# A decoder step: constants issued by GpSimd, eight stage buffers for w_out, the first merged tile in two parts, output stores issued by SyncE

## The reference

```
h = RMSNorm(x);  z = h @ w_in          # pool 512 | 3 x (q, k, v) | gate_pool 1024 | gate_attn 1024
A = (pooling mixer of z) @ w_branch_pool
B = (dilated sliding attention, 3 head groups) @ w_branch_attn
merged = sigmoid(gate_pool) * A + sigmoid(gate_attn) * B
x += RMSNorm(merged @ w_out)
up = RMSNorm(x) @ ffn_w_up;  act = gelu(conv(up)_a) * conv(up)_b
y = x + RMSNorm(act @ ffn_w_down)
```

## Time and profile before

| | |
|---|---|
| three timed runs | 1652.8, 1654.02, 1658.04 us; median 1654.02 us |
| profiled execution | 1652.44 us, of which the span from first to last instruction is 1650.8 us |
| mean granted TensorE clock | 0.982 |
| busy share of the span | PE 97%, PE weight loads 90%, DVE 44%, ACT 33%, POOL 9% |
| chain that ended last | PE 94%, DVE 3%, ACT 1%, issue 1% |

### The profile page before, as it was taken

How to read it: one execution, slowest core, us unless ns; L and a number is a source line. 1 busy time by engine, 2 the same in 40 slices (tenths; PEclk the granted TensorE clock), 3 DMA queues, 4 the chain that set the end, 5 groups by cost and what they waited for, 6 DMA issues and landing times.

```text
span 1650.8 us, 24555 instructions
## 1 busy us (share of the span) xinstructions
PE 1597.7 (97%) x9631; PEld 1485.9 (90%) x9631; DVE 731.7 (44%) x1205; ACT 550.7 (33%) x1058; POOL 146.3 (9%) x193
## 2 busy tenths in 40 slices
PE   6999999999999999979999999999999999999996
PEld 6889999999999999968889999999999998888774
DVE  6474563656322232245444343434343435464533
ACT  7233231333221231133333333333333334343432
POOL 0123242330000000000000000000000000000000
PEclk9999999999899999999999999999999999999998
DMA  7134355340423422040036654655542217565550
GB/s 248 54 107 149 116 186 189 108 148 27 140 77 112 121 91 74 16 164 18 0 107 211 196 175 157 212 191 177 161 150 66 82 48 260 178 218 175 201 164 29
DMA packets 143107, 218.91 MB, mean 133 GB/s; under 512 B 13121, under 2 KB 115953, under 8 KB 142136
## 3 DMA queue, kind: packets, MB, share of 16 engines
q1 hardware_dynamic: 132423, 190.99, 36.5%
q0 software_dynamic: 9648, 26.01, 4.2%
q10 hardware_dynamic: 969, 0.99, 0.2%
HBM read 192.14 MB, written 70.02 MB: 159 GB/s over the span
## 4 chain that ended last, share of the span: by engine, by line
PE 94%; DVE 3%; ACT 1%; issue 1%; DMA 0%; ACTq 0%; POOL 0%; POOLq 0%; DVEq 0%
PE PS L987 48%; PE PS L1195 16%; PE PS L882 9%; PE PS L1123 6%; PE PS L867 4%; PE PS L1051 2%; PE PS L939 2%; PE PS L911 1%; PE PS L925 1%; PE PS L1095 1%; PE PS L895 1%; PE PS L849 0%; PE PS L1132 0%; DMA wo_stage<-in_w_out 0%; PE PS L1002 0%
## 5 line engine op out<-in xcount | busy, mean ns | idle before, releaser
L1729 DVE TENSOR_TENSOR tw_lo<-tw_stage,tw_hi 128x1024 fp32r<-128x1024 f32 x72 | 86.5, 1202 | 415.7 <-ACT tw_hi L1336 415.5
L987 PE MATMUL PS<-h_hi,tw_hi 128*128 128x352 f32 x1032 | 226.1, 327 | 0.0
L987 PE MATMUL PS<-h_hi,tw_lo 128*128 128x352 f32 x1032 | 222.4, 323 | 0.0
L987 PE MATMUL PS<-h_lo,tw_hi 128*128 128x352 f32 x1032 | 221.9, 323 | 0.0
L987 PEld LDWEIGHTS PS<-h_hi,tw_lo 128*128 128x128 f32 x1032 | 176.8, 188 | 0.0
L987 PEld LDWEIGHTS PS<-h_lo,tw_hi 128*128 128x128 f32 x1032 | 175.1, 188 | 0.0
L987 PEld LDWEIGHTS PS<-h_hi,tw_hi 128*128 128x128 f32 x1032 | 173.6, 189 | 0.4
L1995 DVE TENSOR_TENSOR wd_lo<-wd_stage,wd_hi 128x1024 fp32r<-128x1024 f32 x66 | 80.8, 1225 | 137.9 <-ACT as_hi L1526 136.7
L1336 ACT ACTIVATE tw_hi<-tw_stage 128x1024 fp32r<-128x1024 f32 x72 | 72.8, 1012 | 206.7 <-PE PS L987 200.2
L2018 DVE SCALAR_TENSOR_TENSOR cacc<-cext,cols,cacc 128x1024 f32<-128x1024 f32 x88 | 113.0, 1285 | 56.5 <-ACT cacc L1550 27.7
L1195 PE MATMUL PS<-wd_hi,as_hi 128*128 128x512 f32 (+1 forms) x396 | 123.1, 392 | 1.1 <-ACT cnat L1559 1.1
(11 more groups left out here) (253 smaller groups left out, 2717.3 us busy)
## 6 DMA issues: line engine op xcount, KB each, us to landing
wd_stage<-in_ffn_w_down SPq DMA_DIRECT2D x66, 512.0 KB, 3.5
tw_stage<-in_ffn_w_up SPq DMA_DIRECT2D x44, 512.0 KB, 3.9
out_k_s<-in_cache_k_w SPq DMA_DIRECT2D x8, 2044.0 KB
out_v_s<-in_cache_v_w SPq DMA_DIRECT2D x8, 2044.0 KB
qb<-zs SPq DMA_DIRECT2D x24, 512.0 KB, 5.1
acts<-cact POOLq DMA_DIRECT2D x22, 528.0 KB, 8.5
tw_stage<-in_w_in SPq DMA_DIRECT2D x20, 512.0 KB, 5.7
as_stage<-acts SPq DMA_DIRECT2D x44, 192.0 KB, 3.7
```

Of the source, the lines that this page charges most:

```text
L987: last = pe.matmul(PS[:, bank + b, 0:BW], w[s][:, k, :], x[:, k, b * BW:(b + 1) * BW], start=(k == 0 and j == 0), stop=(k == kc - 1 and j ...
L1729: dve.tensor_tensor(tw_lo[s][:, 0:kc, :], tw_stage[s][:, 0:kc, :], tw_hi[s][:, 0:kc, :].bitcast(F32), ALU.subtract).then_inc(tw_lo_done, 1)
```

## The change

1. The eight constants are issued by POOL, just behind the `eps` memset, and no longer by ACT. ACT takes a root of `eps` into a cell that is overwritten later, so that the table with the root is the first one loaded.
2. w_out has eight stage buffers: four new ones lie where `ba_stage` and `tw_stage` were, and are loaded once these have been read (`ba_split` 2; `tw_lo_done` 29 and 30). The loads of x follow behind all eight; the last one waits for four blocks of w_out instead of eight, and the first load of ffn_w_up for all eight.
3. Tile 0 of merged has a place of its own (`mg_first`) and is split in two parts, blocks 0 to 5 and 6 to 7. ACT copies the first part during the last gate block; all eight `split_wo` stand together behind the last gate. PE's tile 0 waits for `ba_used` 7 besides, since the banks that it writes are read by `gated_attn(6)`.
4. At the end DVE multiplies PSUM by the gain as soon as the sum of squares is there, takes the reciprocal, and does the scaling and the addition of x in one instruction. `ytmp` has three buffers. SP issues the stores: three behind load 30, three behind load 52, three at the end.

```diff
@@ SBUF places and buffers
+        BA_STAGE = Y + 2 * 4 * T
+        wo_stage += [at(o)(f"wo_stage{4 + i}", [P, D]) for i, o in enumerate((BA_STAGE, BA_STAGE + 4 * D, TW, TW + 4 * D))]
...
+        mg_first = at(TW + 4 * KC * P * 2)("mg_first", [P, KC, P], F32R)
...
-        ytmp = [sb1(f"ytmp{s}", [P, D]) for s in range(2)]
+        ytmp = [sb1(f"ytmp{s}", [P, D]) for s in range(3)]
@@ sync
             for k in range(KC):
-                if k == KC - 1:
-                    sp.wait_ge(ba_done, KC)
-                    load_x(0)
-                if k >= 4:
-                    sp.wait_ge(wo_lo_done, k - 3)
-                sp.dma_start(wo_stage[k % 4][:, :], w_out[:, k, :]).then_inc(qw_in[k % 4], 16)
+                if k == 4:
+                    sp.wait_ge(ba_split, 2)
+                if k >= 6:
+                    sp.wait_ge(tw_lo_done, 2 * PAIR_UP + k - 6 + 1)
+                sp.dma_start(wo_stage[k][:, :], w_out[:, k, :]).then_inc(qw_in[k] if k < 4 else xr_in[k - 4], 16)
+            sp.wait_ge(ba_done, KC)
+            load_x(0)
             load_x(1)
-            sp.wait_ge(wo_lo_done, KC)
+            sp.wait_ge(wo_lo_done, 4)
             load_x(2)
             sp.dma_start(xnat[0:TS, 8, :], xs).then_inc(x_in[2], 16)
+            sp.wait_ge(wo_lo_done, KC)
...
+            def store_y(n):
+                sp.wait_ge(y_ready, n + 1)
+                dst, part = (ys, slice(0, TS)) if n == 8 else (yp[n * P:n * P + P], slice(0, P))
+                sp.dma_start(dst, ytmp[n % 3][part, :]).then_inc(y_out[n % 3], 16)
             for q in range(NWD, len(DOWN)):
                 load_down(q)
+                if q % FC == 8 and q > FC:
+                    for x in range(3):
+                        store_y(3 * (q // FC - 1) + x)
+            for n in range(6, NTILE):
+                store_y(n)
@@ gpsimd
             pool.memset(eps[:, :], EPS).then_inc(pool_set, 1)
+            for dst, src in ((mask[:, :], io["c_mask"].rearrange("p b k -> p (b k)")), (smask[:, :], io["c_smask"]), (count[:, :, :], io["c_count"]),
+                             (par_a[0:16, :], io["b_gate"][0].rearrange("(j p) -> j p", p=P)),
...
+                pool.dma_start(dst, src).then_inc(const_in, 16)
...
-            for n in range(NTILE):
-                pool.wait_ge(y_ready, n + 1)
-                dst, part = (ys, slice(0, TS)) if n == 8 else (yp[n * P:n * P + P], slice(0, P))
-                pool.dma_start(dst, ytmp[n % 2][part, :]).then_inc(y_out[n % 2], 16)
@@ tensor
                     if n == 0:
                         pe.wait_ge(wo_lo_done, k + 1)
-                        pe.wait_ge(mg_done, 1 if k < KC - 1 else 2)
-                    hi, lo = mg_hi[n % 2][:, k, 0:rows], mg_lo[:, k, t0:t0 + rows]
+                        pe.wait_ge(mg_done, 1 if k < KC - 2 else 2)
+                    if n == 0 and k == 0:
+                        pe.wait_ge(ba_used, KC - 1)
+                    hi, lo = (mg_hi[n % 2] if n else mg_first)[:, k, 0:rows], mg_lo[:, k, t0:t0 + rows]
@@ scalar
             act.dma_start(gb[:, :], io["norm_mix_pre"][0].partition_broadcast(P)).then_inc(gain_in, 16)
-            for dst, src in ((mask[:, :], io["c_mask"].rearrange("p b k -> p (b k)")), (smask[:, :], io["c_smask"]), (count[:, :, :], io["c_count"]),
...
-                act.dma_start(dst, src).then_inc(const_in, 16)
+            act.wait_ge(pool_set, 1)
+            act.activation(rms[:, 0, 0:1], eps[:, 0:1], ACT.Sqrt)
...
-            act.wait_ge(pool_set, 1)
             square(0)
...
                 if j < KC - 2:
                     split_tw(PAIR_GA + j // 2 + 1, j % 2, KC)
-            for k in range(3):
+                if j == KC - 2:
+                    act.wait_ge(tp_done[0], PAIR_UP)
+                    act.wait_ge(sum_done, KC - 2)
+                    act.activation(mg_first[:, 0:KC - 2, :], merged[:, 0:KC - 2, 0:P], ACT.Copy).then_inc(mg_hi_done, 1)
+            for k in range(KC):
                 split_wo(k)
...
-            act.wait_ge(sum_done, KC - 1)
-            act.activation(mg_hi[0][:, 0:KC - 1, :], merged[:, 0:KC - 1, 0:P], ACT.Copy).then_inc(mg_hi_done, 1)
-            for k in range(3, KC):
-                split_wo(k)
             act.wait_ge(sum_done, KC)
-            act.activation(mg_hi[0][:, KC - 1, :], merged[:, KC - 1, 0:P], ACT.Copy).then_inc(mg_hi_done, 1)
+            act.activation(mg_first[:, KC - 2:KC, :], merged[:, KC - 2:KC, 0:P], ACT.Copy).then_inc(mg_hi_done, 1)
@@ vector
+            low_first(0, KC - 2, 1)
             low_wo(0)
+            low_wo(1)
             gated_attn(KC - 2)
...
@@ vector, last stage, for each tile
+                    rows = tile_of(n)[1]
+                    dve.wait_ge(o_ss, 9 + n + 1)
+                    if G:
+                        dve.wait_ge(y_out[x], 16 * G)
+                    dve.tensor_tensor(ytmp[x][0:rows, :], PS[0:rows, 2 * pair:2 * pair + 2, :].rearrange("p b n -> p (b n)"),
+                                      gfin[0:rows, :], ALU.mult).then_inc(f_free, 1)
                     dve.wait_ge(o_rms, 9 + n + 1)
-                    rows = tile_of(n)[1]
                     dve.reciprocal(prstd[0:rows, 1, n:n + 1], prms[0:rows, 1, n:n + 1]).then_inc(f_step, 1)
                     dve.wait_ge(f_step, n + 1)
-                    dve.wait_ge(y_out[n % 2], 16 * (n // 2))
-                    dve.scalar_tensor_tensor(ytmp[n % 2][0:rows, :], PS[0:rows, 2 * pair:2 * pair + 2, :].rearrange("p b n -> p (b n)"),
-                                             prstd[0:rows, 1, n:n + 1], gfin[0:rows, :], ALU.mult, ALU.mult).then_inc(f_free, 1)
                     dve.wait_ge(f_free, n + 1)
-                    dve.tensor_tensor(ytmp[n % 2][0:rows, :], ytmp[n % 2][0:rows, :], xnat[0:rows, n, :], ALU.add).then_inc(y_ready, 1)
+                    dve.scalar_tensor_tensor(ytmp[x][0:rows, :], ytmp[x][0:rows, :], prstd[0:rows, 1, n:n + 1], xnat[0:rows, n, :],
+                                             ALU.mult, ALU.add).then_inc(y_ready, 1)
```

More of the change, by code:

```diff
@@ L488, in build @@
         y_ready = sem("y_ready")
-        y_out = [sem(f"y_out{s}") for s in range(2)]
+        y_out = [sem(f"y_out{s}") for s in range(3)]
         state_out = sem("state_out")
@@ L1440, in split_wo @@
             def split_wo(k):
-                act.wait_ge(qw_in[k % 4], 16 * (4 * NG + k // 4 + 1))
-                act.activation(wo_hi[:, k, :], wo_stage[k % 4][:, :], ACT.Copy).then_inc(wo_hi_done, 1)
+                if k < 4:
+                    act.wait_ge(qw_in[k], 16 * (4 * NG + 1))
+                else:
+                    act.wait_ge(xr_in[k - 4], (80, 48, 48, 48)[k - 4])
+                act.activation(wo_hi[:, k, :], wo_stage[k][:, :], ACT.Copy).then_inc(wo_hi_done, 1)
             act.wait_ge(merge_done, KC + 1)
@@ L1896, in low_wo @@
                 dve.wait_ge(wo_hi_done, k + 1)
-                dve.tensor_tensor(wo_lo[:, k, :], wo_stage[k % 4][:, :], wo_hi[:, k, :].bitcast(F32), ALU.subtract)\
+                dve.tensor_tensor(wo_lo[:, k, :], wo_stage[k][:, :], wo_hi[:, k, :].bitcast(F32), ALU.subtract)\
                    .then_inc(wo_lo_done, 1)
@@ L1917, in _, with low_first @@
             gated_attn(KC - 3)
+            def low_first(lo, hi, part):
+                dve.wait_ge(mg_hi_done, part)
+                dve.tensor_tensor(mg_lo[:, lo:hi, 0:P], merged[:, lo:hi, 0:P], mg_first[:, lo:hi, :].bitcast(F32),
+                                  ALU.subtract).then_inc(mg_done, 1)
+            low_first(0, KC - 2, 1)
             low_wo(0)
+            low_wo(1)
             gated_attn(KC - 2)
-            dve.wait_ge(mg_hi_done, 1)
-            dve.tensor_tensor(mg_lo[:, 0:KC - 1, 0:P], merged[:, 0:KC - 1, 0:P], mg_hi[0][:, 0:KC - 1, :].bitcast(F32),
-                              ALU.subtract).then_inc(mg_done, 1)
-            low_wo(1)
             low_wo(2)
+            low_wo(3)
+            low_wo(4)
             gated_attn(KC - 1)
-            for k in range(3, KC):
-                if k == 4:
-                    dve.wait_ge(mg_hi_done, 2)
-                    dve.tensor_tensor(mg_lo[:, KC - 1, 0:P], merged[:, KC - 1, 0:P], mg_hi[0][:, KC - 1, :].bitcast(F32),
-                                      ALU.subtract).then_inc(mg_done, 1)
-                low_wo(k)
+            low_wo(5)
+            low_first(KC - 2, KC, 2)
+            low_wo(6)
+            low_wo(7)
             def low_merged(n):
```

13 lines of the change are left out of this document (6 added, 7 removed).

## The result

The changed kernel takes 1634.67 us (median of 4 runs, 1631.17 to 1638.46) against 1656.03 us for the kernel before on the same chip (4 runs, 1652.8 to 1658.56): a ratio of 0.9873, 95% interval 0.9842 to 0.9903. The forecast was 1640.0 us with a range of 1636.5 to 1645.5. Repeated later, six runs of the changed kernel gave 1636.77 us against 1656.48 (11 runs), ratio 0.9888 [0.9868, 0.9908]; all ten together have a median of 1636.0 us.

The account below looks back on a forecast made before the run. PE was taken as the bound, busy 97% of the span, so gains come from its stops and both ends: 11.7 + 0.6 + 0.9 = 13.2 us, giving 1640.0 us (middle of 1639.2 and 1640.8), range 1636.5 to 1645.5 us.

Parts of the forecast that it names:

- First output tile, 11.7 us: From the last branch product to tile 1: PE's waits for w_out shrink, tile 1 begins at 727.0 instead of 738.75 us.
- Rival 3: At tile 0 DVE is the bound and the clock falls: gain 9.4 us there, time 1642.3 us; chance 0.08.
- End, 0.9 us: Behind the last matmul: DVE's shorter steps, third buffer and SP's issue bring the last store 0.9 us earlier, bounds 0.3 and 1.6.
- What follows the landing (8.2 us to the end of the span) stays: At the program's close: the 8.2 us between the last store's landing and the span's end were taken as unchanged.
- A: Theory of the follow-up runs: the program closes late, by some 8 us, because GpSimd issued a transfer shortly before the end.
- B: Theory of the follow-up runs: the shorter close has a cause not tied to who issues the store.
- Start, 0.6 us: Ahead of PE's first product: earlier squares by ACT bring 0.6 us, range -1.5 to 4.0 us.
- the bound of -1.5: At the start, lower bound: constants moved beside the gain's load may cost 1.8 us, less the 0.33 us gained.
- rival 2: The constants delay the start, which loses 1.5 us instead of gaining 0.6: time 1642.1 us; chance 0.12.
- the 0.33 us that the forecast saw in the square's row: At the start: ACT's square of tile 1 at 10.95 instead of 11.28 us, the gain that reaches PE this way.
- Rival 1: Clock in the gate loop: shifted beginning worsens passes, up to 6 us more or 2 less; 1644 to 1646 us; chance 0.15.
- Rivals 4 and 5: 4: SP's stores delay down-projection weights, slower than before, chance 0.02; 5: start gains most of 4 us, 1637 us, chance 0.08.

Follow-up runs that it names:

- the two kernels above: Kernel before with the w_out part alone (buffers, order, two-part merged tile): 1643.83 us; kernel before with the eight stage buffers and their loads alone: 1646.92 us.

## Why the prediction was right and wrong

*First output tile, 11.7 us: right.* Measured 11.96 and 11.92 us. DVE's steps, the place of the remaining wait (the sixth block) and the clock came as worked out; the wait was 1.0 us where 1.4 and then 0.2 were counted, and the part of `mg_lo` took 0.42 us (0.45). The buffers alone gave 9.4 us of it and the order with the two parts 2.6 us, as the two kernels above show. The stop ahead of tile 0 is gone. Rival 3 is refuted: PEclk stayed at 1.00.

*End, 0.9 us: the step that failed.* Its first half was right: the last store is issued 3.80 us behind the last matmul instead of 4.86, 1.06 us gained where 0.9 were forecast. The failed step is the sentence "What follows the landing (8.2 us to the end of the span) stays". It did not: the end came 2.5 us behind the issue instead of 10.4, 7.9 us more, and 0.6 us behind the landing instead of 8.2. The 8.2 us had been read as a property of the program's end, although its row named the engine, and nobody asked what else in those 8.2 us depended on POOL. Four kernels with GpSimd issuing last show the same 10.4 us; with GpSimd's issue moved back 2.5 us, 9.9 us from it; moved back to 93 us ahead of the end, nothing. So A holds, and a cause without GpSimd (B) is out. By what mechanism GpSimd's issue holds up the close stays open. Taken from the kernel before on the same chip (1656.03 us) the forecast gain of 13.2 us gives 1642.8 us; the measured 1634.67 us are 8.2 us less, about this one term.

*Start, 0.6 us: wrong in sign, small in size.* The list of what is late next was right in kind (the fourth w_in block, then tile 1's square), and the bound of -1.5 held. The failed step is that gain and fourth block would land as before, at 8.3 and 10.6 us. They landed 0.9 and 0.5 us later, which is rival 2, "the constants delay the start", at a fraction of its price of 1.5 us: the mean over profiles is a loss of 0.2 us, within their spread. By the Trainium skill ("DMA: Bandwidth & Descriptors", "SWDGE vs HWDGE vs iDMA") the DMA engines take turns between GpSimd's queue and the others; the landing times above, and their recovery once the constants wait, agree with it, though no run tells turns from any other way of sharing. That the table load at the head, without GpSimd's constants, is worth 0.9 us was more than the 0.33 us that the forecast saw in the square's row.

*Rival 1, the clock in the gate loop: real, and not the change's.* It cost the first profile 7.7 us against the second. But the same program had 51.2 us on the lower level in one profile and 34.1 in another, and of all 14 profiles eight had 34.1 us (the kernel before among them), two 41.0, one 44.4 and three 51.2. The forecast tied it to a shift of the loop's beginning; yet the profile with the q/k product at 50.00 us (tiles 6 and 7 by POOL) had 51.2 us, and those with 49.95 and 50.03 us (the changed kernel again, the end alone) had 34.1. What picks the pattern stays open. It moves single runs: the changed kernel's from 1630.77 us (mean clock 0.988) to 1639.29 (0.982).

*Rivals 4 and 5: did not happen.* No wait of PE in the down projection but the 1.1 us for `cnat` (the rows of the convolution's state) that was there before. SP's first three stores (1.52 us of issuing; the next three took 2.58) stood where the forecast put them:

```profile
1459.30 1.52 SPq L737 DMA_DIRECT2D out_y_prompt<-ytmp  x3
1461.23 0.34 SPq L724 DMA_DIRECT2D wd_stage<-in_ffn_w_down  x1
```

These stores are slow all the same: three at once in SP's queue landed 8.0 and 7.6 us (medians, first and second pass) behind their issue, where POOL's, 2.7 us apart, took 2.9 us both before and in the kernel with tiles 3 to 5 by POOL. Nothing waits for them that long, and the weights' loads beside them took 3.7 and 4.9 us where they took 3.7 and 3.9.

*The sum.* 13.2 us were forecast. The profiles at equal clock give 21.7: +0.2 at the tile, +0.2 in the last steps, +7.9 at the close, -1.25 at the start, and +1.45 of clock, which the change did not cause. Here -1.25 is the stretch ahead of the branch's end, 0.65 us lost where 0.6 were to be gained. Without the close the errors are -0.85 us, and +0.6 us with the clock: within 1 us of the forecast.

## What to carry to other kernels

Ask of the stretch behind the last row of a timeline, too, what it hangs on: if it is long, look who issued the last transfers, and let SP issue the late ones instead of GpSimd. How early GpSimd's last issue must lie is not known from here: 9.9 us ahead of the end of the span it still held up the close, 93 us ahead it did not. When a term is "and the rest stays", it needs a reason as the others do. At a start that is bound by landings, moving small loads to an idle engine is no gift: those that PE waits for land later, so put the small ones behind them.

## What the runs showed of the hardware

- The span ended 10.4 us behind GpSimd's last DMA issue in four kernels where that issue was the last, 9.9 us where SP's came 2.5 us later, and 2.5 us behind SP's last issue where GpSimd's lay 93 us or more ahead of the end of the span. Nothing between 9.9 and 93 us was tried, nor ACT as the last issuer, nor what the close does in that time.
- A 1.0 us and a 1.35 us stop of PE left the granted clock at 1.00 here. The 6.99 us stop was followed by 0.74, and one of 7.21 us at the same place, in the kernel with the end alone, by 0.71. A wait of 1.1 us at the start of the down projection was followed by 0.66 in two profiles (the kernel before, the buffers alone) and by 1.00 in the other twelve, so the length of the stop alone does not decide it.
- One program can run its loop of small matmuls with 34 to 51 us on the lower clock level, which moved the span by 7.7 us, a little less than half of the 17.1 us.
- Three stores of 512 KB issued at once by SP beside the weights' loads landed after 7.6 to 8.0 us, single ones by GpSimd beside the same loads after 2.9 us.
